# Selection marks, the dilated attention's second head and stage borders in a two-layer hybrid trunk

## The reference, cut to what matters

```python
# even_mixer -> dsa_attention, for a block of 128 queries
logits = jnp.einsum('bqhd,bkd->bqhk', qi, k_idx)
score = jnp.einsum('bqh,bqhk->bqk', wi, jax.nn.relu(logits))
visible = kpos[None, :] <= qpos[:, None]
score = jnp.where(visible[None], score, -jnp.inf)
_, sel = lax.top_k(score, topk)          # topk = 256
...
# odd_mixer
q = rope(rmsnorm(q.reshape(B, S, N_HEADS_C, HEAD_DIM), qn_c), pos)
k = rope(rmsnorm(k.reshape(B, S, N_HEADS_C, HEAD_DIM), kn_c), pos)
return dilated_attention(q, k, v).reshape(B, S, -1) @ w_out
```

## Time and profile before

| | us |
|---|---|
| median of 3 runs | 3275.99 (3271.0 to 3277.57) |
| the profiled execution | 3274.92 |
| its span, first to last instruction | 3273.1 |
| TensorE busy | 3164.6 (97%) |
| VectorE busy | 1822.0 (56%) |
| ScalarE busy | 1265.9 (39%) |
| GpSimd busy | 769.1 (23%) |

### The profile page before, as it was taken

The page is one execution under the profiler, slowest core; times in us unless marked ns, Lnnn a source line. Parts: engine busy times, 40 slices in busy tenths (PEclk is TensorE's granted clock), DMA queues, the critical chain, the costliest instruction groups (busy, mean ns, idle before and its releaser), DMA issues. The chain is left out here.

```text
span 3273.1 us, 44702 instructions
## 1 busy us (share of the span) xinstructions
PE 3164.6 (97%) x15622; PEld 2653.9 (81%) x15622; DVE 1822.0 (56%) x3084; ACT 1265.9 (39%) x2724; POOL 769.1 (23%) x478
## 2 busy tenths in 40 slices
PE   7889998999999999999999999999999999999999
PEld 6668887988878888888887887899778888888887
DVE  5499998888344444444443331899434444444452
ACT  4285426877232222222332211788332222222241
POOL 3015444564200000000122543776210000000030
PEclk9899999999999999999999999999999999999999
DMA  5313333122222111211111334233212121112021
GB/s 172 114 55 94 99 118 98 45 64 78 84 65 64 38 51 38 64 39 38 41 63 39 100 103 140 58 67 75 70 40 65 39 61 41 51 39 64 19 65 52
DMA packets 268603, 221.93 MB, mean 68 GB/s; under 512 B 82844, under 2 KB 220876, under 8 KB 268492
## 3 DMA queue, kind: packets, MB, share of 16 engines
q1 hardware_dynamic: 268492, 220.49, 22.9%
HBM read 173.80 MB, written 46.14 MB: 67 GB/s over the span
## 5 line engine op out<-in xcount | busy, mean ns | idle before, releaser
L1960 DVE TENSOR_SCALAR_CACHE_REDUCE k_x<-k_x,l0in_cand,l0in_want 128x384 bf16<-128x384 f32 (+1 forms) x186 | 174.9, 1003 | 1.2 <-DVE l0in_before L1955 0.2
L2189 DVE SCALAR_TENSOR_TENSOR l0ff_c<-l0ff_g,l0ff_cw,l0ff_c 128x512 f32<-128x512 f32 x44 | 33.1, 752 | 254.9 <-ACT l0ff_c L2094 254.9
L2189 DVE SCALAR_TENSOR_TENSOR l1ff_c<-l1ff_g,l1ff_cw,l1ff_c 128x512 f32<-128x512 f32 x44 | 33.1, 752 | 254.9 <-ACT l1ff_c L2094 254.9
L2164 POOL TENSOR_TENSOR l0pg_x_lo<-l0pg_raw,l0pg_x_hi 128x1024 fp32r<-128x1024 f32 x4 | 9.6, 2404 | 669.8 <-ACT l0pg_x_hi L2143 669.8
L2164 POOL TENSOR_TENSOR l1pg_x_lo<-l1pg_raw,l1pg_x_hi 128x1024 fp32r<-128x1024 f32 x4 | 9.6, 2404 | 669.8 <-ACT l1pg_x_hi L2143 669.8
L2180 DVE TENSOR_TENSOR k_x<-l0ff_d,k_x 128x512 f32<-128x512 f32 x176 | 119.2, 688 | 76.7 <-PE l0ff_d L74 76.6
L2180 DVE TENSOR_TENSOR k_x<-l1ff_d,k_x 128x512 f32<-128x512 f32 x176 | 119.2, 688 | 76.7 <-PE l1ff_d L74 76.6
L72 PE MATMUL l1in_acc<-k_w_lo,k_hi 128*128 128x512 f32 x384 | 151.4, 394 | 3.1 <-PEq L114 3.0
L73 PE MATMUL l1in_acc<-k_w_hi,k_lo 128*128 128x512 f32 x384 | 150.6, 392 | 0.0
L74 PE MATMUL l1in_acc<-k_w_hi,k_hi 128*128 128x512 f32 x384 | 150.5, 392 | 0.0
L72 PE MATMUL l0ff_gu<-k_lo,l0ff_w_hi_g 128*128 128x512 f32 x352 | 137.0, 389 | 3.1 <-PEq L2275 3.1
(11 more groups left out here) (493 smaller groups left out, 9649.6 us busy)
## 6 DMA issues: line engine op xcount, KB each, us to landing
l0w_raw<-in_w_in_even SPq DMA_DIRECT2D x24, 512.0 KB, 4.6
k_raw<-in_w_in_odd SPq DMA_DIRECT2D x24, 512.0 KB, 4.4
l0ff_raw_g<-in_w_gate SPq DMA_DIRECT2D x22, 512.0 KB, 4.0
l0ff_raw_u<-in_w_up SPq DMA_DIRECT2D x22, 512.0 KB, 5.3
l0ff_raw_d<-in_w_down SPq DMA_DIRECT2D x22, 512.0 KB, 4.9
l1ff_raw_g<-in_w_gate SPq DMA_DIRECT2D x22, 512.0 KB, 4.0
l1ff_raw_u<-in_w_up SPq DMA_DIRECT2D x22, 512.0 KB, 5.3
l1ff_raw_d<-in_w_down SPq DMA_DIRECT2D x22, 512.0 KB, 4.8
```

The lines of the kernel that those rows point to most:

```text
L1960: tick(dve.tensor_scalar(hits[:, cols], score[:, cols], cand[:, i:i + 1].bitcast(F32), want[:, i:i + 1], ALU.is_ge, ALU.add, accum_out=exc ...
L2164: pool.tensor_tensor(n_lo, nxt.raw[:, n % 2, :, :], n_hi.bitcast(F32), ALU.subtract).then_inc(n_lo_ready, 1)
L2189: dve.scalar_tensor_tensor(c[:, half, :], g[:, at - 1:at + 511], cw[:, 1, bass.ds(blk, 1)], c[:, half, :], ALU.mult, ALU.add).then_inc(con ...
```

## The change

The causal mask is loaded earlier, in the indexer, and copied into the last 128 columns of each score strip before the first accumulation, in place of the additions in the selection. Masked scores are now allowed to follow the sign, so the counts that are wanted are worked out from the strip's `width` and no longer from `seen`; the diagonal corrections go. The marks are built from the scores below the level with 2 to the 100th (`BAR`) as the unit, and one fused operation writes them. The six sign multiplications are no longer waited for one by one. For the dilated attention, `Staging` gets a place of its own for the second head (`second_at`, in the region that is the merged output's later), the projection stage before loads, scales and rotates it behind the first head, and the attention is called with staged=2. `recycle` has no barrier any more: numbers that were cleared one border earlier are freed, and the stage's own ones are cleared by GpSimd at the start of the next stage, in contiguous ranges. Left out below are renamings (`seen`, `above`) and the callers that pass the new arguments.

```diff
@@ -62,9 +63,9 @@
-    seen = (np.arange(P)[:, None] + P * np.arange(TSEL, NT)[None, :] + 1).astype(np.float32)
+    width = np.broadcast_to(P * np.arange(TSEL + 1, NT + 1), (P, NT - TSEL)).astype(np.float32)
...
-            "c_seen": seen}
+            "c_width": np.ascontiguousarray(width)}
@@ -109,9 +111,14 @@
-    nc.clear_and_free_semaphores(list(Stage.used))
+    nc.extend_free_semaphores(Stage.cleared)
+    Stage.cleared = sorted(h.num for h in Stage.used)
...
-    nc.all_engine_barrier()
+    first = Stage.cleared[0]
+    for last, following in zip(Stage.cleared, Stage.cleared[1:] + [0]):
+        if following != last + 1:
+            nc.gpsimd.sem_clear(range(first, last + 1))
+            first = following
@@ -502,8 +510,9 @@
-                    next_head.load(sp, 0, 0, n_raw_in)
+                    next_head.load_ahead(sp, 0, n_raw_in[0])
...
+                    next_head.load_ahead(sp, 1, n_raw_in[1])
@@ -575,10 +584,14 @@
-                next_head.scaled_ahead(pool, 0, n_raw_in, n_step)
+                next_head.scaled_ahead(pool, 0, n_raw_in[0], n_step)
...
-                next_head.rotate(pool, 0, n_step, 8)
+                next_head.rotate(pool, next_head.stage[0], n_step, 8)
+                pool.wait_ge(n_step, 12)
+                next_head.scaled_ahead(pool, 1, n_raw_in[1], n_step)
+                pool.wait_ge(n_step, 14)
+                next_head.rotate(pool, next_head.second_stage, n_step, 14)
@@ -1049,13 +1062,17 @@
-    def __init__(self, st, proj, q_at, k_at, q_gain, k_gain, rstd, q_grp, k_grp, rope, decay, gains_at):
+    def __init__(self, st, proj, q_at, k_at, q_gain, k_gain, rstd, q_grp, k_grp, rope, decay, gains_at, second_at=None):
...
+        self.second_raw, self.second_stage = self.raw[1], self.stage[1]
+        if second_at is not None:
+            self.second_stage = place("second_stage", [2, NT, 2, HD], second_at)
+            self.second_raw = place("second_raw", [2, NT, HD], second_at + 8 * KB)
@@ -1066,8 +1083,14 @@
+        self.load_into(sp, self.raw[b], h, arrived)
+    def load_ahead(self, sp, h, arrived):
+        self.load_into(sp, self.second_raw if h else self.raw[0], h, arrived)
+    def load_into(self, sp, raw, h, arrived):
...
-            sp.dma_start(self.raw[b][:, i, :, :],
+            sp.dma_start(raw[:, i, :, :],
@@ -1078,9 +1101,10 @@
+        raw = self.second_raw if b else self.raw[0]
...
-            pool.tensor_tensor(self.xn[:, i, :, :], self.raw[b][:, i, :, :],
+            pool.tensor_tensor(self.xn[:, i, :, :], raw[:, i, :, :],
@@ -1448,15 +1472,16 @@
-            def turn(item, b, bank):
+            def turn(item, b, bank, second=False):
...
+                staged_head = head.second_stage if second else stage[b]
...
-                        src = stage[b][:, "qk".index(kind), t, :, :].rearrange("p c d -> p (c d)")
+                        src = staged_head[:, "qk".index(kind), t, :, :].rearrange("p c d -> p (c d)")
@@ -1647,6 +1672,7 @@
+            sp.dma_start(first.mask[:], first.consts["mask"]).then_inc(mask_in, 16)
@@ -1707,6 +1733,10 @@
+            dve.wait_ge(mask_in, 16)
+            for t in range(T0, NT):
+                dve.tensor_copy(score[:, sel_at(t + 1) - P:sel_at(t + 1)], first.mask[:, P:2 * P]).then_inc(barred, 1)
+            dve.wait_ge(barred, NT - T0)
@@ -1926,28 +1955,23 @@
-            dve.wait_ge(const_in, 48)
+            dve.wait_ge(const_in, 32)
...
-                diag = slice(cols.stop - P, cols.stop)
...
-                link(dve.tensor_tensor(score[:, diag], score[:, diag], causal, ALU.add))
...
-            link(dve.scalar_tensor_tensor(want[:], seen[:], float(2 * TOPK - 1), tmp[:], ALU.subtract, ALU.mult))
-            link(dve.tensor_tensor(want[:], want[:], seen[:], ALU.subtract))
+            link(dve.scalar_tensor_tensor(want[:], width[:], float(2 * TOPK - 1), tmp[:], ALU.subtract, ALU.mult))
+            link(dve.tensor_tensor(want[:], want[:], width[:], ALU.subtract))
...
-                diag = slice(cols.stop - P, cols.stop)
-                link(dve.tensor_scalar(score[:, cols], score[:, cols], sign[:, i:i + 1], None, ALU.mult))
-                link(dve.scalar_tensor_tensor(score[:, diag], causal, 4.0, score[:, diag], ALU.mult, ALU.add))
+                tick(dve.tensor_scalar(score[:, cols], score[:, cols], sign[:, i:i + 1], None, ALU.mult))
+            dve.wait_ge(step, n[0])
@@ -1976,17 +2000,15 @@
-                diag = slice(cols.stop - P, cols.stop)
-                s, at = score[:, cols], level[:, i:i + 1]
+                s, at, need = score[:, cols], level[:, i:i + 1], tmp[:, i:i + 1]
...
-                link(dve.scalar_tensor_tensor(score[:, diag], causal, 8.0, score[:, diag], ALU.mult, ALU.add))
-                tick(dve.tensor_scalar(above[:, 0:w], s, at, 0.0, ALU.is_gt, ALU.add, accum_out=cnt[:, i:i + 1]))
-                link(dve.tensor_scalar(eq[:, 0:w], s, at, None, ALU.is_equal))
-                link(dve.tensor_scalar(tmp[:, i:i + 1], cnt[:, i:i + 1], -1.0, float(TOPK), ALU.mult, ALU.add))
+                tick(dve.tensor_scalar(below[:, 0:w], s, at, 0.0, ALU.is_lt, ALU.add, accum_out=cnt[:, i:i + 1]))
+                link(dve.tensor_scalar(eq[:, 0:w], s, at, -BAR, ALU.is_equal, ALU.mult))
+                tick(dve.tensor_scalar(cnt[:, i:i + 1], cnt[:, i:i + 1], float(TOPK - w), -BAR, ALU.add, ALU.mult))
...
-                link(dve.scalar_tensor_tensor(junk[:, 0:w], junk[:, 0:w], tmp[:, i:i + 1], eq[:, 0:w], ALU.is_le, ALU.mult))
-                link(dve.tensor_tensor(above[:, 0:w], above[:, 0:w], junk[:, 0:w], ALU.add))
-                link(dve.tensor_scalar(s, above[:, 0:w], 1.0, -NEG, ALU.subtract, ALU.mult))
+                link(dve.tensor_tensor(need, cnt[:, i:i + 1], junk[:, w - 1:w], ALU.add))
+                link(dve.scalar_tensor_tensor(junk[:, 0:w], junk[:, 0:w], need, eq[:, 0:w], ALU.is_lt, ALU.mult))
+                link(dve.scalar_tensor_tensor(s, below[:, 0:w], -BAR, junk[:, 0:w], ALU.mult, ALU.add))
@@ -2326,7 +2349,8 @@
-                    dil = Staging(mix, proj, 0, 1024, a["q_norm_c"][0], a["k_norm_c"][0], stats, 0, 16, a["c_rope"], None, SMALL_AT + 352)
+                    dil = Staging(mix, proj, 0, 1024, a["q_norm_c"][0], a["k_norm_c"][0], stats, 0, 16, a["c_rope"], None, SMALL_AT + 352,
+                                  second_at=MERGED_AT + 8 * KB)
@@ -2345,7 +2369,7 @@
-                                    mask_load=(sliding[:], a["c_mask"][1]), v_written=vstored, next_out=out_buf)
+                                    mask_load=(sliding[:], a["c_mask"][1]), staged=2, v_written=vstored, next_out=out_buf)
```

More of the change, by code:

```diff
@@ L30 @@
 NEG = -1e30
+BAR = 2.0 ** 100
 DIL = ((128, 1), (512, 4), (2048, 16))
@@ L81 @@
     used = []
+    cleared = []
     zone = 0
@@ L481, in projection_stage @@
                     slot=buf.slot, first=AHEAD, first_root=ROOTS)
-        n_tab_in, n_raw_in, n_step = (st.sem(n) for n in ("n_tab_in", "n_raw_in", "n_step"))
+        n_tab_in, n_step = st.sem("n_tab_in"), st.sem("n_step")
+        n_raw_in = [st.sem(f"n_raw_in{b}") for b in range(2)]
         raw_in = [st.sem(f"raw_in{b}") for b in range(2)]
@@ L1101, in tables_ahead, with rotate @@
             pool.tensor_tensor(self.sin_g[:, i, :, half:HD], self.cs[:, 1, :, half:HD], bc(i, 0, half), ALU.mult).then_inc(step, 1)
-    def rotate(self, pool, b, step, n):
+    def rotate(self, pool, stage, step, n):
         half = HD // 2
@@ L1111, in rotate @@
         twice = lambda x: flat(x).unsqueeze(2).to_broadcast([P, 2 * NT, 2, HD])
-        pool.tensor_tensor(self.stage[b][:, :, :, :, :].rearrange("p i t c d -> p (i t) c d"), twice(self.ra), twice(self.rb),
+        pool.tensor_tensor(stage[:, :, :, :, :].rearrange("p i t c d -> p (i t) c d"), twice(self.ra), twice(self.rb),
                            ALU.add).then_inc(step, 1)
@@ L1220, in _ @@
             if next_head is not None:
-                next_head.load(sp, 0, 0, n_raw_in[0])
+                next_head.load_ahead(sp, 0, n_raw_in[0])
                 next_head.load_tables(sp, n_tab_in)
@@ L1240, in _ @@
                 sp.wait_ge(raw_free, nh)
-                next_head.load(sp, 1, 1, n_raw_in[1])
+                next_head.load_ahead(sp, 1, n_raw_in[1])
             if next_out is not None:
@@ L1276, in body @@
                 else:
-                    head.rotate(pool, b, pool_step, at + 2)
+                    head.rotate(pool, stage[b], pool_step, at + 2)
                     pool.wait_ge(pool_step, at + 6)
@@ L1297, in _ @@
                 pool.wait_ge(n_step, 14)
-                next_head.rotate(pool, 1, n_step, 14)
+                next_head.rotate(pool, next_head.second_stage, n_step, 14)
             if next_out is not None:
@@ L1521, in body @@
                                 pe.wait_ge(stage_ready, h + 1)
-                            turn(item, 1 - b, n % 3)
+                            turn(item, 1 - b, n % 3, second=first)
                     for ahead, g, i in order.logits.get(item, ()):
```

(14 more changed lines are left out.)

## The result

The kernel after takes 3247.1 us in the median of 6 runs (3244.4 to 3251.9), the kernel before 3276.3 (6 runs, 3271.0 to 3279.5). The ratio is 0.9915, interval 0.9904 to 0.9927. The forecast was 3258, range 3252 to 3266: the sign and the three mechanisms hold, the size is too small. In the profiled pair, 3274.92 against 3248.09 us, it is 26.8 us where the sum said 17.7.

The account below looks back on a forecast made before the run. TensorE was busy 97% of the span, so only its standstills could be won: 5.7 + 6.3 + 7.0 - 0.3 - 1.0 = 17.7 us off the profiled 3274.92 gives 3257.2, as a median 3258 us, range 3252 to 3266.

Parts of the forecast that it names:

- Part 1: Ten borders between stages: without the second barrier each is 0.63 us shorter, less 0.6 for clears; 5.7 us saved.
- The 0.3 given back twice: Two ConvGLU stage starts: TensorE waits for GpSimd behind its semaphore clears, charged 0.3 us at each.
- Part 2: Border before layer 0's forgetting attention: VectorE's selection chain ends about 12 us earlier, gain capped by SP's store; 6.3 us saved.
- the release comes at 507.2 instead of 513.5: Border before the forgetting attention: engines are let go 0.4 us after SP's last store at 506.8; 6.3 us earlier.
- rival a: Forgetting attention's border: VectorE still ends last as its small operations meet GpSimd's; half the term kept, 3261.5 us, chance 0.07.
- Part 3: Indexer's start: the mask's transfer ahead of the keys' copies delays them; 0.3 us lost.
- the cover: Indexer: six mask copies, 1.8 us, fit into the 5.90 us that VectorE idles before its first accumulation.
- Part 4: Layer 1's dilated attention: second head made ready in the projection before, so TensorE's wait for GpSimd goes; 7.0 us saved.
- Part 5: TensorE's half-clock stretches after standstills: 0 in the dilated attention, a costlier stretch at the forgetting attention; 1.0 us lost.
- the one at 675: Half-clock stretch of TensorE from 675 to 682 with 6.22 us busy, taken as model for the dilated attention; 0 change.

Follow-up runs that it names:

- the first trace: The first profiled execution of the unchanged kernel before, from which the prediction was made: 3274.92 us.
- the pauses: Kernel after with 18 TensorE pauses in the ConvGLU stages, of one, four or twelve GpSimd memsets each: 3269.8, 3306.9 and 3426.8 us.

## Why the forecast was too small

- **Part 1, borders (5.7).** Right in its mechanism. 4.7 in the profiled pair: 0.5 to 0.8 at nine, -1.0 at the last. There GpSimd is last, with a weight rest (L2186) that ends 1.8 us behind TensorE's last matmul; that border is 1.7 to 2.6 us in the old form, and in the new one 1.1 to 1.5 in six traces and 3.0 to 3.1 in three, the profiled one among them. The 0.3 given back twice for the clears ahead of the ConvGLU stages was not needed: those borders fell by 0.6 us like the rest. Alone the part gave 7.8 us (3.6 to 10.2), with the embedding stages' 1.4 in it, a term that the forecast did not have.
- **Part 2, selection (6.3).** The mechanism and the cap are right: the chain gave 14.6 us (277.6 to 263.0) where 12 were forecast (6.2 for 7 ahead of the search, 9.7 for 5 in the marks, and a search 1.3 longer), and the release moved by what SP's store allowed. The step "the release comes at 507.2 instead of 513.5" holds for that execution, so it adds nothing to the error in the profiled pair; but the other four traces of the unchanged stage stood still 14.3 to 15.0 us, and the usual gain is about 10. That the pair fits is partly luck: the first trace had the short chain, and an indexer 1.2 us longer than the mean of the four others. I named the phase between the two engines, and the search's small operations in it, but only as a danger for the time after (rival a), not as a spread of the time before.
- **Part 3, indexer (-0.3), a step that failed.** The charge was sized well (0.5: the wait for the keys' copies is 3.2 instead of 2.7 us), and the cover held: the six copies took 0.90 us together, half of the 1.8. But moving the mask was taken as free for the place that the transfer left: with the mask no longer ahead of the weights, the wait for head 2's queries fell from 2.6 to 1.0 us, and the indexer is 2.8 us shorter in the pair, 1.6 on the means. I looked at what a moved transfer is put in front of, not at what it is taken away from.
- **Part 4, dilated head (7.0).** The length is right, no wait is left of it. In the other traces of the old form the same wait was 6.7 to 8.2 us, shorter where more of head 0 ran at half clock, since GpSimd's work sets the release; the stage's 278.9 to 279.6 us hardly move.
- **Part 5, clock (-1.0), the step that failed most.** "In the dilated attention the half stretch now covers the standstill; without it I expect a stretch like the one at 675, with about as much busy time as now, so 0": it measured 3.4 us busy against 2.83 + 6.56, by the estimate a gain of 3.0, and the stage saved 2.3 us above the standstill (1.7 on the means). At the forgetting attention the work at half clock grew as forecast, 3.50 us to 3.50 + 3.40, which would cost 1.7 us by the estimate, but the stage is only 0.3 us longer (153.5 to 153.8). Over the kernel the estimate gives a gain of 4.9 us in the first pair and 7.3 on the mean of two. I had taken the stretches as fixed things with more or less work in them; in the pauses and in the dilated attention a shorter standstill had less half clock behind it, or none.

The first pair adds up by the table: borders 4.7, chain 6.3, dilated attention 9.3, indexer 2.8, all other stages 3.8, together 26.9 for 26.8. Against the 17.7 of the forecast the indexer gave 3.1 more, the dilated attention 2.3, the borders 1.0 less, and the stages for which the clock was to cost 1.0 saved 3.8. Of these 3.8, 2.0 are the embedding stages; the rest is the sum of gains and losses of up to 1.7 us which follow the half-clock stretches in part. What remains open is what shortens the embedding stages, how often the chain is the short one (1 of 5 traces), and what decides where a stretch at half clock falls in the stages without any standstill.

## What to carry to other kernels

Price a standstill of TensorE among dense matmuls at its length and, at the 7 us measured here, 2.4 us more for the matmuls behind it at half clock; at 1 us, its length alone; at 3 us, half clock followed in 3 of 18 cases. Where other engines set the pace too, as in the sparse attention, half clock costs less than half of the busy time under it. Before you cap a gain by one engine's last end in a trace, ask whether that engine's chain meets another's at random, and take more than one execution, since the trace may be the lucky one. Of a moved transfer count both places: whom it now delays, and whom it no longer does.

## Unexpected on the hardware

- A program and its copy differ by 4.2 us in one VectorE chain of 280 us (277.6 and 281.8). An operation on 128x6 takes 2.28 us instead of 0.17 when it starts just behind one of GpSimd, and 1.09 becomes 3.13 us for 128x896.
- TensorE's standstill of 7.2 us brought half clock behind it every time in the two ConvGLU stages (18 of 18), 2.6 us in 3 of 18, 0.9 us never; 128x512 matmuls then start every 0.43 instead of 0.23 us.
- Semaphore clears at the head of a stage, 17 of 0.17 us in the middle, cost nothing that the borders show, not even in the two stages where TensorE waits for GpSimd behind them.
